# An early first gather, 1/rms inside the input's transposing product, and expert weights in a ring of eight 2 MiB units

## The reference

```python
z = rms_norm(x, g1) @ w_in                       # 1024 -> 5120
A = (rg_lru(causal_conv4(xa)) * gelu(ga)) @ w_proj_a
B = (gelu(u) * (tril(w_s) @ layer_norm(gelu(v)) + b_s)) @ w_proj_b
x = x + (sigmoid(gate_a) * A + sigmoid(gate_b) * B) @ w_out
h = rms_norm(x, g2)
top_logits, top_idx = top_k(h @ w_router + b_router, 4)      # of 32 experts
for each expert e, on its rows hb of h:
    gate, up = split(hb @ w_gate_up[e] + b_gate_up[e])       # 1024 -> 2048
    act = (clip(up) + 1) * gate * sigmoid(1.702 * gate)
    out = act @ w_down[e] + b_down[e]                        # 1024 -> 1024
x = x + sum over the 4 experts of gate weight * out
y = rms_norm(x, g_final)
```

## Time and profile before

| | us |
|---|---|
| median of 3 runs (1251.33 to 1254.01) | 1253.89 |
| profiled execution | 1252.89 |
| its span | 1251.2 |
| PE busy in the span | 1195.1 |
| DVE / ACT / POOL busy | 398.1 / 228.1 / 78.2 |

### The profile page before, as it was taken

One profiled execution on the slowest core, in us unless ns is written; L12 is line 12 of the kernel. 1 busy time (PEld: TensorE's weight loads), 2 busy tenths in 40 slices (PEclk: granted clock), 3 DMA queues, 4 the chain that ended last, 5 costly groups with the idle time before them and its releaser, 6 DMA issues.

```text
span 1251.2 us, 16027 instructions
## 1 busy us (share of the span) xinstructions
PE 1195.1 (96%) x6327; PEld 676.9 (54%) x6327; DVE 398.1 (32%) x641; ACT 228.1 (18%) x391; POOL 78.2 (6%) x235
## 2 busy tenths in 40 slices
PE   5999999998999999989999999999999999998896
PEld 4999999986435354443535444343544435353432
DVE  5547586755223223121312212111221211121123
ACT  5443682123101010000101011010100101010102
POOL 5000000010101010001101010010101101010000
PEclk9999999998999999999999999999999999999898
DMA  8434326585999999999999999999999999999994
GB/s 253 145 116 133 101 84 227 192 317 231 421 422 421 421 421 421 420 421 420 421 421 422 420 422 421 421 420 421 420 418 421 420 421 421 421 421 421 418 421 186
DMA packets 74143, 443.68 MB, mean 355 GB/s; under 512 B 7404, under 2 KB 7500, under 8 KB 24848
## 3 DMA queue, kind: packets, MB, share of 16 engines
q1 hardware_dynamic: 72832, 439.44, 86.3%
q0 software_dynamic: 1232, 3.20, 1.0%
HBM read 440.62 MB, written 1.98 MB: 354 GB/s over the span
## 4 chain that ended last, share of the span: by engine, by line
PE 78%; SPq 10%; DMA 7%; issue 2%; DVE 1%; ACT 1%; DVEq 0%
PE ps L1400 28%; PE ps L1428 16%; SPq L377 10%; PE ps L1332 7%; PE ps L1132 7%; PE ps L1134 7%; DMA wexp<-in_w_gate_up_dram 7%; PE ps L1133 7%; PE ps L1349 2%; PE ps L1392 1%; PE ps L1350 1%; PE ps L1380 1%; PE ps L1213 1%; PE ps L1341 1%; DMA raw<-in_w_in_dram 1%
## 5 line engine op out<-in xcount | busy, mean ns | idle before, releaser
L1400 PE MATMUL ps<-wexp,xt 128*64 128x512 f32 (+1 forms) x2304 | 482.4, 596 | 16.1 <-DMA wexp<-in_w_gate_up_dram 16.1
L1400 PEld LDWEIGHTS ps<-wexp,xt 128*64 128x64 f32 (+1 forms) x2304 | 152.9, 134 | 319.7 <-issue 319.7
L1428 PE MATMUL ps<-wexp,act_t 128*64 128x512 f32 (+1 forms) x1152 | 238.9, 597 | 5.0 <-issue 4.2
L1428 PEld LDWEIGHTS ps<-wexp,act_t 128*64 128x64 f32 (+1 forms) x1152 | 91.8, 134 | 138.7 <-issue 137.7
L1060 DVE TENSOR_TENSOR y<-y,ps 128x1024 f32<-128x1024 f32 x51 | 60.7, 1218 | 228.7 <-PE ps L1350 221.9
L680 ACT ACTIVATE g<-g 128x512 f32<-128x512 f32 x34 | 21.4, 630 | 561.9 <-DVE g L1073 561.9
L1132 PE MATMUL ps<-act_h,split_h 128*128 128x384 f32 x352 | 117.9, 335 | 0.0
L1134 PE MATMUL ps<-act_h,split_l 128*128 128x384 f32 x352 | 117.6, 334 | 0.0
L1133 PE MATMUL ps<-act_l,split_h 128*128 128x384 f32 x352 | 117.6, 334 | 0.0
L1332 PEld LDWEIGHTS ps<-pick,xn 128*128 128x128 f32 x816 | 95.1, 196 | 14.2 <-issue 13.0
L1332 PE MATMUL ps<-pick,xn 128*128 128x128 f32 x816 | 98.3, 282 | 1.1 <-DVE pick L970 1.1
(11 more groups left out here) (281 smaller groups left out, 789.6 us busy)
## 6 DMA issues: line engine op xcount, KB each, us to landing
wexp<-in_w_gate_up_dram SPq DMA_DIRECT2D x256, 1024.0 KB, 23.2
wexp<-in_w_down_dram SPq DMA_DIRECT2D x128, 1024.0 KB, 24.6
raw<-in_w_in_dram SPq DMA_DIRECT2D x20, 1024.0 KB, 5.1
raw<-in_w_proj_a_dram SPq DMA_DIRECT2D x4, 1024.0 KB, 6.1
raw<-in_w_out_dram SPq DMA_DIRECT2D x4, 1024.0 KB, 5.0
raw<-in_w_proj_b_dram SPq DMA_DIRECT2D x2, 1024.0 KB, 6.8
out_dram<-y SPq DMA_DIRECT2D x3, 512.0 KB
x_in<-in_x_prompt_dram SPq DMA_DIRECT2D x2, 512.0 KB, 3.7
```

What stands on the lines that cost most here:

```text
L1400: i_ = pe.matmul(ps[s0:s0 + w, b, :], xt[:, k, s0:s0 + w], wexp[(unit + experts * k + x) % RINGS][:, UC * b:UC * b + UC], start=False, sto ...
L1428: i_ = pe.matmul(ps[s0:s0 + w, 6 + c, :], act_t[:, k, s0:s0 + w], wexp[(unit + experts * (CB + m) + x) % RINGS][:, D * kk + UC * c:D * kk ...
```

## The change

1. **Input.** There is no `xs` as an operand. DVE writes a diagonal matrix `scale` of 1/rms for each token tile (identity times a column), and PE multiplies `x_in` by it, so that the product both turns and scales. It goes tile by tile as the tiles arrive. The state load stands behind the first mixer unit on SP, and all of POOL's loads wait for that unit. The states and `ws_raw` are turned between the two halves of the v product. The first `split_l` is made in quarters, and the first half of the v product goes quarter by quarter.
2. **First gather.** Positions and picks of the first two token tiles are made as soon as their masks are; banks 2 and 3 are opened by a product with zeros, and the gather's products for tiles 0 and 1 stand among the third tile's router work; only the third tile's eight stand behind its pick. DVE evacuates the first half, ACT the second. The bias product of every pass stands behind k=0, and in pass 0 `token_gates(0)` and the gate transposes too.
3. **Ring.** Eight slots of 2 MiB. A gate-up unit holds two adjacent rows of the weight for each partition (16 KB), a down unit four (16 KB); 6 units an expert. `wexp_used` rises after every second k step of gate-up and every fourth of down. The rows of `xn2` are permuted by `normalise` to match. The very last units are loaded in two halves. Of the first eight units, unit 3 waits for the last `split_l`, unit 4 for the last unit but one, and 5 to 7 for the last unit of the mixer.

```diff
-RING_AT = (65536, 73728, 81920, 90112, 155648, ... 139264, 147456)
+RING_AT = (65536, 81920, 155648, 49152, 0, 16384, 32768, 139264)
-EXP_U = 12
+GU_U, DN_U = 4, 2
+EXP_U = GU_U + DN_U
-        wgu = w_gate_up.rearrange("o e (k p) n -> (o e) k p n", p=P)
-        wdn = w_down.rearrange("o e (m p k) n -> (o e) m p (k n)", k=2, p=P)
+        wgu = w_gate_up.rearrange("o e (m p k) n -> (o e) m p (k n)", k=2, p=P)
+        wdn = w_down.rearrange("o e (m p k) n -> (o e) m p (k n)", k=4, p=P)
...
-            sp.dma_start(state_in[0:24, :], ...).then_inc(rows_loaded, 16)
-            sp.dma_start(state_in[24:32, :], ...).then_inc(rows_loaded, 16)
+                if n == 0:
+                    sp.dma_start(state_in[0:24, :], ...).then_inc(state_loaded, 16)
+                    sp.dma_start(state_in[24:32, :], ...).then_inc(state_loaded, 16)
...
             pool.wait_ge(zeroed, 2)
+            pool.wait_ge(mix_landed[0], 16)
+            pool.dma_start(n2p..., norm2_g...).then_inc(n2p_loaded, 16)
...
+            def turn_input(t, cs):
+                pe.wait_ge(scale_ready, t + 1)
+                for c in cs:
+                    i_ = pe.matmul(ps[:, c, t * P:(t + 1) * P], x_in[:, t, c * P:(c + 1) * P], scale[:, t, :], start=True, stop=True)
+                    if t == TT - 1:
+                        i_.then_inc(xs_turned, 1)
+            turn_input(0, range(0, 7))
+            pe.wait_ge(rows_loaded, 7 * 16)
+            pe.transpose(ps[:, 7, T:T + ROWS], rows[:], ident[0:ROWS, 0:ROWS]).then_inc(rows_turned, 1)
+            turn_input(1, range(0, 7))
+            pe.wait_ge(rows_copied, 1)
+            turn_input(0, range(7, 8))
+            turn_input(1, range(7, 8))
+            turn_input(2, range(0, 8))
...
+            def first_tokens(t, cs):
+                pe.wait_ge(xn2_ready, t + 1)
+                if t < 2:
+                    pe.wait_ge(pick_early, t + 1)
+                else:
+                    pe.wait_ge(pick_ready, 1)
+                for c in cs:
+                    i_ = pe.matmul(ps[:, 2 + c // 4, c % 4 * P:(c % 4 + 1) * P], xn2[:, t, c * P:(c + 1) * P], pick[:, t],
+                                   start=False, stop=t == TT - 1 and c % 4 == 3)
+                    if t == TT - 1 and c % 4 == 3:
+                        i_.then_inc(gathered, 1)
+            count_before(0)
+            count_before(1)
             turn_tokens(1, 2)
+            for b in (2, 3):
+                pe.matmul(ps[:, b, :], ones_b[:], zero_b[:], start=True, stop=False)
+            first_tokens(0, range(0, 3))
...
+            first_tokens(0, range(3, 8))
+            first_tokens(1, range(0, 1))
+            count_before(2)
+            first_tokens(1, range(1, 8))
+            first_tokens(2, range(0, 8))
...
                 for k in range(CB):
-                    for x in range(experts):
-                        landed(experts * k + x)
+                    if k % 2 == 0:
+                        for x in range(experts):
+                            landed(experts * (k // 2) + x)
...
-                    i_.then_inc(wexp_used, experts)
+                    if k % 2 == 1:
+                        i_.then_inc(wexp_used, experts)
+                    if k == 0:
+                        pe.wait_ge(sel_ready, it + 1)
+                        for b in range(4):
+                            i_ = pe.matmul(ps[:, b, :], sel[:], bias_hl[:, UC * b:UC * b + UC], start=False, stop=False)
+                        i_.then_inc(sel_used, 1)
+                        if first:
+                            token_gates(0, 7)
...
```

More of the change, by code:

```diff
@@ L97 @@
 LOGIT_BANKS = (4, 5, 7)
-POS_BANKS, COUNT_BANK = (4, 5, 1), 0
+POS_BANKS, COUNT_BANK = (4, 1, 0), 5
 def hawk_gmlp_moe_streaming_step(
@@ L371, in _, with load_pass @@
             sp.wait_ge(order_ready, 1)
-            def load_pass(unit, later, ids, ring):
+            def load_pass(unit, later, ids, ring, last=False):
                 for n in range(EXP_U * len(ids)):
@@ L698, in _ @@
             act.wait_ge(stored, 5 * 16)
-            evacuate_tokens(0, (0, 1))
+            act.wait_ge(n2p_loaded, 16)
+            act.wait_ge(gathered, 2)
+            for c in range(4, CB):
+                i_ = act.activation(xt[:, c, :], ps[:, 3, (c - 4) * P:(c - 3) * P], ACT.Copy, scale=n2p[:, c:c + 1])
+            i_.then_inc(xt_ready, 2)
+            act.preload_act_table(ACT.Silu)
             for it in range(LAST):
@@ L750, in _ @@
-            dve.tensor_copy(h0, turned[:, :, 24:32]).then_inc(rows_copied, 1)
-            low(0)
-            for k in range(2):
-                dve.wait_ge(ws_turned, k + 1)
-                dve.tensor_copy(wst[:, k].rearrange("p g t -> p (g t)"), ps[:, 6 + k, :]).then_inc(ws_ready, 1)
+                dve.wait_ge(squared, t + 1)
+                link(dve.tensor_scalar(st8[:, 4 + t:5 + t], st8[:, t:t + 1], 1.0 / D, RMS_EPS, ALU.mult, ALU.add))
+                dve.reciprocal(st8[:, 4 + t:5 + t], st8[:, 4 + t:5 + t]).then_inc(rstd_in, 1)
@@ L764, in _ @@
             low(1)
+            dve.wait_ge(state_turned, 1)
+            turned = ps[:, 3, 0:CB * 32].rearrange("p (c r) -> p c r", r=32)
+            dve.tensor_copy(samp_pad[:, :, :, 0:CW - 1], turned[:, :, 0:24].rearrange("p c (b k) -> p c b k", k=CW - 1))
+            dve.tensor_copy(h0, turned[:, :, 24:32]).then_inc(state_copied, 1)
+            for k in range(2):
+                dve.wait_ge(ws_turned, k + 1)
+                dve.tensor_copy(wst[:, k].rearrange("p g t -> p (g t)"), ps[:, 6 + k, :]).then_inc(ws_ready, 1)
             low(2)
@@ new lines, in _ @@
+                for j in range(KB):
+                    if h == 0:
+                        if j < KB - 1:
+                            pe.wait_ge(low_first, j + 1)
+                        else:
+                            pe.wait_ge(low_done, 1)
+                    if h == 0 or j == 0:
+                        for t in range(TT):
+                            if h == 0:
+                                pe.wait_ge(xn_ready, max(j, t) + 1)
+                            for jj in (range(j, j + 1) if h == 0 else range(KB)):
+                                ts_ = slice(t * P, (t + 1) * P)
+                                i_ = three(ps[:, t, :], act_h[:, KB * h + jj, ts_], act_l[:, KB * h + jj, ts_],
+                                           split_h[:, h, jj, :], split_l[:, h, jj, :], h == 0 and jj == 0, h == 1 and jj == KB - 1)
+                            if t == TT - 1 and (h == 1 or j == KB - 1):
+                                i_.then_inc(unit_used, 1)
+                            elif h:
+                                i_.then_inc(v_mm, 1)
@@ L1432, in experts_pass @@
                             i_.then_inc(last_mm, 1)
-                    if not last or m < CB // 2 - 1:
+                    if not last or m < DN_U - 1:
                         i_.then_inc(wexp_used, experts)
-            gather(0)
-            token_gates(0)
-            pe.wait_ge(gat3_ready, 1)
-            for t in range(TT):
-                i_ = pe.transpose(ps[0:3 * NE, 6, t * P:(t + 1) * P], gat3[:, t].rearrange("p k e -> p (k e)"), ident[:])
-            i_.then_inc(post_mm, 1)
             for it in range(LAST):
```

247 lines of the change are left out of this document (134 added, 113 removed).

## The result

| | before | after |
|---|---|---|
| median, us | 1253.70 (1251.33 to 1255.37, 20 runs) | 1258.58 (1254.69 to 1262.96, 20 runs) |
| profiled execution / its span | 1252.89 / 1251.2 | 1255.52 / 1253.8 |
| PE waits for weights | 16.1 us in 15, longest 1.5 | 19.0 us in 11, longest 2.7 |

The ratio is 1.0045, 95% interval [1.0037, 1.0053]: slower by 4.9 us, where 1245.5 and faster were forecast.

A forecast was written before the change was run, and what follows sets the result against it. DMA and PE were taken as both nearly full in the passes, PE as the bound ahead of them. 1252.9 - 3.5 (input) - 4.8 (gather) + 0.9 (ring) = 1245.5 us, range 1233 to 1256.

The forecast's parts named there:

- Input: Kernel start: first product at 14.0 us, z chunks from 34.2 instead of 37.69, 3.5 us gained; unit 1 and `ws_raw` just in time.
- I am wrong if `v` stops PE in the first 40 us: Kernel start: the forecast's warning that it fails if unit 1, `ws_raw` or `v` stops PE in the first 40 us.
- First gather: Before the passes: first expert product 7.1 us earlier, less 2.35 for work moved behind k=0, net 4.8 us gained.
- Rate: Expert passes: 16 KB rows lift the DMA from 421 to 429 GB/s; 1 GB/s worth some 1.7 us.
- the rivals at 421 and 425: Passes: DMA at 421 GB/s gives 1258 us, chance 0.11; at 425 GB/s 1252, no change, chance 0.11.
- Coarser ring: Passes: PE's waits for weights sum to 17.0 us against 16.1, a net cost of 0.9 us with the better rate.
- (a): First expert product to step k=6 of pass 4: PE waits 8.6 us, where 6.0 was; step reached after 248.7.
- (b): After a solo pass the DMA stands still 2.0 us; PE waits 1.4 by step 6 of pass 9 (2.3 before).
- (c): From pass 11 to step 6 of pass 15: PE waits 7.0 us for weights (7.8 before).
- The rival "clock": Passes or gather: the clock falls at PE's longer waits, 3 to 6 us on top, 1250 us; chance 0.13.
- The rival on the other side: Passes: rate stays at 421 GB/s, waits 29.7 us, 1258 us, slower than before; chance 0.11.

The follow-up runs named there:

- experiment 5: Changed kernel, but POOL issues its recurrence weights and layer-norm rows only after mixer unit 2 has landed: 1253.74 us, ratio 1.0006.
- experiment 6: Changed kernel with the old ring (16 slots of 1 MiB, 8 KB rows) and POOL's loads behind mixer unit 2: median 1246.43 us, short group 1245.9.
- experiment 2: Kernel before with the early first gather alone (and the bias product behind k=0): 1248.69 us, ratio 0.9968.
- experiment 7: Kernel before with the early gather alone, pass 0's bias, gates and transposes moved behind the fifth to seventh weight step: 1252.04 us, ratio 0.9994.
- experiment 3: Changed kernel with its ring of 2 MiB units, each read as two 8 KB rows per partition instead of one of 16 KB: 1267.17 us, ratio 1.0111.
- experiment 4: Changed kernel with the input stage of the kernel before; early gather and new ring kept: 1255.43 us, ratio 1.0024.
- experiment 1: Changed kernel with the ring of before (16 slots of 1 MiB, 8 KB rows); new input and early gather kept: 1249.52 us, ratio 0.9984.

## Why the prediction was wrong

**Input: the first step that failed, a load taken as just in time that was not.** The bottleneck and the chain of `v` were right, the transfers beside them not. The first product came at 15.7 (14.0 forecast; unit 0 landed at 12.4 and not at 10.6). What cost the gain stood one unit further. The prediction looked at what the DMA carries together with unit 0, and let "POOL's loads" simply come later; later meant beside unit 2. That unit came 2.2 us late, DVE stood idle 1.83 us before its low part, and `v` came late with it (36.19, forecast 34.2); unit 3, which ACT must round before it reads `v`, landed only at 32.9, so that with unit 2 alone in time `v` would by these times still come at 36.1 (32.9 + 1.9 to round + 1.3 to load a table). PE's wait of 3.06 us, where the forecast's own times leave 1.7, was followed by some 3.4 us at half clock (0.66 over 5 us). The step read -3.5 and measured +1.0 to the mixer's end in the profiled execution (289.83, before 288.83); as medians it costs 0.8 (within the scatter) with the ring of sixteen and 3.1 with that of eight. That POOL's loads are the cause of the wait is shown by experiments 5 and 6: with one wait on POOL it is 1.1 to 1.3 us in all seven traces, and z is at 34.8 to 35.8 in six of them, forecast 34.2. The medians fall by 4.8 and 3.1 us; with the ring of eight the traces show about 1 of that. "I am wrong if `v` stops PE in the first 40 us" was the right warning with no chance of its own in the sum.

**First gather: right.** 7.3 us against 7.1 from the mixer's end, 4.2 against 4.8 in the time. Of the 7.3 the moved work was forecast to take 2.35; the traces have 3.1 (from the first expert product to the end 948.9 in experiment 2, 945.8 before). Why these 0.7 is open; experiment 7, meant for it, showed another thing.

**Rate: right in size, wrong in worth.** Forecast 429 in the windows, measured 427 to 429; the rivals at 421 and 425 fell. The Trainium skill (DMA: Bandwidth & Descriptors, "Where 436 GB/s comes from") puts the end at 435.2; by it the trace agrees, for no slice passed 431. The 425 of the Trainium skill's section "Measured" on the same page is 2 to 4 GB/s under the trace, and the trace decides. What the rate was worth is another matter: 240 MiB between step 6 of pass 4 and of pass 15 took 602.7 us (548.99 to 1151.66), 417.6 GB/s on the mean, less than the 418.8 before. Experiment 3, the same ring with rows of 8 KB, puts the worth of the long rows at 8.6 us, not 12.7.

**Coarser ring: the larger step that failed.** "The ring costs 0.9 us net; the better rate and the coarser steps cancel" measured 7 us: as medians 6.7 (experiments 4 and 2), 7.8 (5 and the short group of 6) and 9.1 (the changed kernel and 1), and 6.6 in the profiled executions (954.7 from the first expert product to the end, where 945.8 + 2.35 stood before). The other traces agree: with the early gather, its work where the change has it, and the ring of sixteen seven of them have 948.6 to 949.8 us there, with the ring of eight and long rows seven have 954.1 to 956.5. By experiment 3 the grain costs about what the formulas say and the rate pays back too little; the cancelling failed. Of its three terms:

- (a) Step 6 of pass 4 came 249.9 after the first expert product, forecast 248.7; the waits were 7.9 (8.6 forecast), and 1.6 went to a group at half clock.
- (b) The forecast let the DMA stand still 2.0 us in a light pass. From the windows 620 to 660 it moved 14.5 MB where 428 GB/s make 17.1: 6.2 us' worth are missing, and some 6 again around 900. Only 638 to 640 is empty; the rest are shorter pauses from 624 on, while PE gives back one slot after another in the solo pass. All seven traces with the ring of eight and long rows have 359 to 362 GB/s there, those with the ring of sixteen in the same place 421 or 422. PE's waits in pass 9 were 3.7 us, not 1.4.
- (c) Passes 14 and 15: 7.4 us of waits and 1.7 for a group at half clock, where 7.0 was forecast.

The waits alone, 19.0 against 17.0, look nearly right. The rest is what waits of 2.2 to 2.7 us bring: two groups at 8.7 instead of 7.1, 3.3 us. The rival "clock" had priced that at 3 to 6 us, and held it for another case than the forecast; it was a part of every case with 2 MiB units, since pairs of them make the waits long: each of the eight traces with such units has one to four of these groups ahead of the last pass, those with 1 MiB units have none there.

**The rival on the other side** had the right sign by the wrong cause: 1258 from a rate of 421, which the windows exclude. The change was slower at 428.

**What stays open.** The profiled executions of the changed kernel (1254.6 to 1256.9, five of them) add up by these steps; its median is 1258.6, and what adds the other 2 to 3 us no trace shows. And the kernels with the new input and the ring of sixteen had 11 of 36 runs some 10 to 11 us above the rest, at a mean clock of 0.986 to 0.990 instead of 0.990 to 0.994, where those with the early gather, the old input and that ring had none in 17, and the kernel before none in 79 (1251.1 to 1256.1). The lower clock is measured; what makes it fall in them, and where, no trace shows. It can't be all: by an estimate from these figures a mean of 0.990 instead of 0.994 is 10 us more at half clock, which cost some 5 us and not 10. In the changed kernel too the times don't follow the clock strictly (1261.2 and 1261.6 at 0.983, but 1260.1 at 0.990 and 1263.0 at 0.988).

## What to carry to other kernels

A ring has two sizes, its bytes and its grain: halving the number of slots at the same bytes cost 14 us here in the traces and 18 by the medians, by pauses when light work gives slots back slowly and by waits nearly twice as long, and 1.7% of rate paid back 8.6; price both before trading one for the other. A small load that is moved out of the way of a critical one is moved in the way of the next: write down what is in flight at its new place. And before a piece of work is pushed back on PE, follow what its consumer engine has queued behind it; 13.7 us of delay for the gates became a stop of all loads.

## What the runs showed that was not expected

- The rate by row length, with the DMA engines full: 421 GB/s for 8 KB rows (share 1.01), 427 to 429 for 16 KB. The line through 4 and 8 KB rows forecast that to within 2 GB/s.
- POOL's seven loads of small rows (L431 to L435) beside two 1 MiB loads stretched them from 5.1 and 5.4 us to 7.3 and 9.4.
- A wait of PE of 2.7 us was followed by half clock in some executions and by full clock in others, at the same step; waits for weights of 1.9 us or less by full clock. The changed kernel spreads over 8 us where the one before spreads over 4; the traces explain 2 of them.
